# One transformer step with RWKV, linear attention and attention: the first RWKV batch is merged like the others, modulated rows are scaled at the residual, and turned modulation rows wait for the next ones

## The chip, the cores and the metric

The kernel runs on 1 core of one Trainium2 chip. The metric is device time in microseconds, from one launch, of that core. Three runs of the kernel before gave 2029.8, 2041.27 and 2041.91 us; their median is 2041.27 us.

## The reference

Two layers (`DEPTH = 2`) of a hybrid backbone run over 384 tokens: 128 context tokens and 256 latent tokens, each a row of 1024 channels. Cut to what matters:

```python
mod = silu(cond) @ w_ada + b_ada            # shift, scale and gate of both sub-layers
h = rms_norm(x, g_mix) * (1 + sc1) + sh1
p = h @ w_in
o_a = attention(...)                        # 8 heads, QK-norm, rotary
o_b = gated linear attention, forward + backward
o_c = RWKV-7 scan, forward + backward, group norm, gate
merged = sum of sigmoid(gate_i) * (o_i @ w_po_i)
x = x + gt1 * (merged @ w_out)
h2 = rms_norm(x, g_ffn) * (1 + sc2) + sh2
x = x + gt2 * ((silu(gu[:F]) * gu[F:]) @ w_ffn_out)
```

The outputs are the new rows of x and the context's keys, values and final states. All is float32; the six large projections are computed as three products of rounded halves (high x high, low x high, high x low).

## The kernel before

Channels lie on the 128 partitions and the 384 tokens along the free axis, so x and h are 8 tiles of 128x384. The program is written out by hand for each engine (`@block.tensor`, `@block.vector` and so on), and every hand-over is a semaphore; nothing is scheduled by a tool. A layer has five phases with a barrier behind each: (0) input projection, (1) attention, (2) gated linear attention, (3) RWKV, (4) output projection and feed-forward.

**Weights.** SyncE streams them in a fixed order into a ring of three slots of 1 MB. A slot is loaded again when its last user is done (`last_use`). The large projections split each arrived chunk into a high and a low half (ACT copies at L1361, DVE subtracts at L1816).

**Side work.** The matmuls of the branch gates (`gate`, L624, 8 matmuls of 128x384 in 4 steps), of the branch projections (`po`, L630, 4 matmuls in 2 steps) and of the modulation (`ada`, L621, one step each) have no place of their own: a generator `side_steps` hands them out in the order of `side_plan`, and the PE program calls `fill(n)` for n steps wherever it would wait. In RWKV the counts stand in the tuple `FILLS`, taken in turn by `fill(next(steps))`. The 48 steps of phase 3 are po 0 to 3 with gates between, four ada, po 4 to 7 with gates between, four ada. Two PSUM banks (6 and 7) serve all of it alternately, so a step that begins a new item waits until the item two before it is emptied. The side results are taken out by ACT (ada to `modrow`, L1340; gates, L1353) and by DVE (po, L1808 and L1810; modulation, L1801), each in `side_work`, which runs at fixed points of their programs, ahead of the next ordinary bank they take over.

An ada step gives 256 modulation values as a row; `turn_mod` (L603) turns them to columns by two small matmuls. `modrow` has two halves, so ACT takes row j only when row j-2 has been turned. The row is turned when more than two are held behind an ada item, and at once behind an item of another kind:

```python
while len(rows) > (2 if kind == "ada" else 0):
    turn_mod(*rows.pop(0))
```

**RWKV (phase 3).** The 8 heads go in 4 batches of 2 heads, n = 0 to 3, and each batch has both directions d = 0, 1 over 6 chunks of 64 tokens. For each of the 8 groups g = 2n + d DVE and ACT form decay terms (`logs` L2101 to L2105, `keys` L2113 to L2116, `terms` L2125 to L2137). Then follow for each batch: `grams` (PE L883, DVE L2146 to L2153), `begin` (DVE transpose L2159), a substitution on POOL (`substitution`, L1279 to L1286), `inverses` (DVE L2164, L2169, L2173), `merges` (PE L990 and L999 with DVE and ACT taking out each of the steps MM, QQ, SS, EE, FF), `factor` (PE L932, L943; DVE L2239; ACT L1604), `values` (PE L524, L958), `turned` (L969) and `read` (L990), `transitions` (PE L990 and L999), three `scan_step`s (PE L1034, DVE L2208) with fills between them, and `outputs` (PE L1047, L1053). For n = 1 and 2 factor, values, turned and read stand inside `merges`, where for n = 0 and 3 there are fills. For n = 0 they stand ahead of the loop, and for n = 3 at the end of batch 2.

**Norm.** The squares of x go to `squared` (for the first norm of a layer that is h itself; ACT, L1383), are summed over channels by ones-matmuls (L549), and ACT makes rstd in `gate[:, 0]` by Ln and Exp (L1391, L1393). DVE then makes h = x * scale * rstd for each of the 8 tiles in two pieces, 128 context and 256 latent columns, since the two have different scales (L1844); ACT writes the high half with the shift added (L1372) and DVE the low half (L1824). `residual` (L1855, L1856) adds gt * projection to x, one tile at a time, in the output projection and the second feed-forward projection.

## Time and profile before

| | us |
|---|---|
| runs, median of 3 | 2041.27 |
| the profiled execution | 2040.51 |
| its span, first to last instruction | 2038.7 |
| PE busy (90%) | 1826.6 |
| DVE busy (50%) | 1025.7 |
| ACT busy (36%) | 736.7 |
| POOL busy (7%) | 149.4 |

The phases are found in the trace by their lines. Layer 0: start to 48, input projection to 208, attention to 298, linear attention to 403, RWKV to 648, output and feed-forward to 1047 us. Layer 1: 1206, 1298, 1402, 1645 and the end. In the rows a line number is one of the kernel, "out<-in" are tiles, x is a count, and the bracket is the idle time of the engine just ahead with what ended it. PE rows may cover many matmuls; one float32 matmul is recorded as two instructions, so one step of a gate is x4. A busy time is no rate: at half the granted clock the same matmuls fill twice the time.

### The profile page before, as it was taken

Reading aid. Unit: us, or ns where it says so; the run is one execution under the profiler, and the core shown is the slowest. Engines: PE = TensorE matmul, PEld = TensorE weight load, DVE = VectorE, ACT = ScalarE, POOL = GpSimd, SP = SyncE. Lnnn points to the kernel's source line nnn. Section 1 sums busy time; section 2 is a strip of 40 time slices with the busy share of each in tenths; the row PEclk is TensorE's granted clock in tenths of the full one; section 3 lists DMA queues with packets and bytes.
Section 4 is the critical chain, followed back from the end, with each engine's and each line's share of the span. In section 5 each row is a group of like instructions: output and inputs, shape, how many; then the busy total and the mean of one; then the engine's idle time right before and its main releaser. Section 6 shows DMA issues by size and latency. Waiting matters only on the chain.

```text
span 2038.7 us, 38816 instructions
## 1 busy us (share of the span) xinstructions
PE 1826.6 (90%) x16819; PEld 1544.8 (76%) x16819; DVE 1025.7 (50%) x1827; ACT 736.7 (36%) x1297; POOL 149.4 (7%) x325
## 2 busy tenths in 40 slices
PE   5899898878796999999989989888687989999998
PEld 2899455546564989999989975555466669899998
DVE  1426438888544453333342444597775345533332
ACT  2334434333233343333243443523332333433321
POOL 2000000034110000000000000000522000000000
PEclk8899999989798999999999999999888989999999
DMA  7443231201304444663443433311012234344342
GB/s 259 166 127 114 89 110 47 81 9 44 105 3 145 145 135 131 185 166 106 128 134 106 126 96 100 111 51 47 2 61 89 84 117 127 94 126 130 112 116 85
DMA packets 267937, 214.48 MB, mean 105 GB/s; under 512 B 7226, under 2 KB 259545, under 8 KB 267513
## 3 DMA queue, kind: packets, MB, share of 16 engines
q1 hardware_dynamic: 264816, 204.41, 33.1%
q0 software_dynamic: 2736, 7.54, 1.2%
q8 instruction: 134, 2.20, 0.5%
q14 instruction: 35, 0.28, 0.0%
q10 hardware_dynamic: 216, 0.06, 0.0%
HBM read 209.10 MB, written 2.88 MB: 104 GB/s over the span
## 4 chain that ended last, share of the span: by engine, by line
PE 72%; DVE 17%; ACT 5%; issue 4%; DMA 1%; SPq 0%; ACTq 0%; POOL 0%; DVEq 0%; POOLq 0%
PE bank L565 12%; PE bank L570 12%; PE bank L566 12%; PE bank L624 8%; PE bank L1188 3%; PE bank L1186 3%; PE bank L1187 3%; PE bank L990 3%; DVE gate L2076 3%; PE bank L621 2%; PE bank L630 2%; PE bank L524 1%; PE bank L999 1%; PE bank L932 1%; PE bank L603 1%
## 5 line engine op out<-in xcount | busy, mean ns | idle before, releaser
L566 PE MATMUL bank<-scr_rounded 128*128 128x384 f32 x1344 | 453.6, 337 | 0.0
L566 PEld LDWEIGHTS bank<-scr_rounded 128*128 128x128 f32 x1344 | 254.9, 190 | 1.3
L565 PE MATMUL bank<-scr_rounded,gate_rounded 128*128 128x384 f32 (+1 forms) x672 | 229.0, 341 | 12.7 <-ACT scr_rounded L1372 9.5
L565 PE MATMUL bank<-scr_rounded 128*128 128x384 f32 (+1 forms) x672 | 227.0, 338 | 9.2 <-ACT scr_rounded L1372 8.7
L624 PE MATMUL bank<-h,ring 128*128 128x384 f32 x576 | 218.8, 522 | 10.9 <-DVEq L351 9.6
L570 PE MATMUL bank<-scr_rounded,gate_rounded 128*128 128x384 f32 (+1 forms) x672 | 223.2, 338 | 0.0
L570 PE MATMUL bank<-scr_rounded 128*128 128x384 f32 (+1 forms) x672 | 221.8, 336 | 0.0
L1816 DVE TENSOR_TENSOR scr_rounded<-ring,gate_rounded 128x2048 fp32r<-128x2048 f32 (+3 forms) x65 | 135.4, 2083 | 159.1 <-ACT gate_rounded L1361 158.4
L1816 DVE TENSOR_TENSOR scr_rounded<-ring,scr_rounded 128x2048 fp32r<-128x2048 f32 (+1 forms) x65 | 135.4, 2083 | 144.3 <-ACT scr_rounded L1361 143.7
L624 PEld LDWEIGHTS bank<-h,ring 128*128 128x128 f32 x576 | 108.7, 200 | 92.1 <-issue 38.0
L1361 ACT ACTIVATE gate_rounded<-ring 128x2048 fp32r<-128x2048 f32 (+3 forms) x65 | 113.6, 1747 | 153.2 <-PE bank L570 67.9
L1361 ACT ACTIVATE scr_rounded<-ring 128x2048 fp32r<-128x2048 f32 (+1 forms) x65 | 113.5, 1746 | 146.9 <-PE bank L570 84.5
L565 PEld LDWEIGHTS bank<-scr_rounded,gate_rounded 128*128 128x128 f32 (+1 forms) x672 | 127.9, 190 | 15.5 <-issue 11.0
L565 PEld LDWEIGHTS bank<-scr_rounded 128*128 128x128 f32 (+1 forms) x672 | 126.9, 189 | 10.9 <-issue 9.3
L570 PEld LDWEIGHTS bank<-scr_rounded,gate_rounded 128*128 128x128 f32 (+1 forms) x672 | 127.3, 190 | 0.5
L570 PEld LDWEIGHTS bank<-scr_rounded 128*128 128x128 f32 (+1 forms) x672 | 126.3, 189 | 0.6
L2380 DVE TENSOR_TENSOR arena<-bank,arena 128x384 f32<-128x384 f32 x44 | 24.5, 558 | 170.5 <-PE bank L570 166.5
L630 PE MATMUL bank<-arena,ring 128*128 128x384 f32 x256 | 97.4, 518 | 6.3 <-DVEq L351 4.1
L621 PE MATMUL bank<-ring,scond 128*2 128x256 f32 x768 | 57.7, 423 | 24.3 <-ACT modrow L1340 13.5
L630 PEld LDWEIGHTS bank<-arena,ring 128*128 128x128 f32 x256 | 47.4, 197 | 37.1 <-issue 12.3
L830 PEld LDWEIGHTS bank<-scr 64*128 64x128 f32 x672 | 42.1, 188 | 36.2 <-DVE scr L2058 21.6
L830 PE MATMUL bank<-scr 64*128 64x128 f32 x672 | 50.6, 287 | 18.5 <-DVE scr L2058 11.0
(386 smaller groups left out, 3180.0 us busy)
## 6 DMA issues: line engine op xcount, KB each, us to landing
ring<-in_w_in_dram SPq DMA_DIRECT2D x56, 1024.0 KB, 5.3
ring<-in_w_ada_dram SPq DMA_DIRECT2D x48, 1024.0 KB, 5.2
ring<-in_w_ffn_in_dram SPq DMA_DIRECT2D x88, 512.0 KB, 5.3
ring<-in_w_ffn_out_dram SPq DMA_DIRECT2D x32, 704.0 KB, 4.6
ring<-in_w_out_dram SPq DMA_DIRECT2D x8, 1024.0 KB, 5.0
ring<-in_w_po_a_dram SPq DMA_DIRECT2D x4, 1024.0 KB, 6.0
ring<-in_w_po_b_dram SPq DMA_DIRECT2D x4, 1024.0 KB, 6.2
ring<-in_w_po_c_dram SPq DMA_DIRECT2D x4, 1024.0 KB, 9.8
```

What stands on the lines that cost most here:

```text
L565: pe.matmul(o, w_hi[:, k, :], right[0][k], start=k == 0, stop=False)
L566: pe.matmul(o, w_lo[:, k, :], right[0][k], start=False, stop=False)
L570: ins = pe.matmul(o, w_hi[:, k, :], right[1][k], start=False, stop=k == nk - 1)
L621: ins = pe.matmul(b[strip:strip + 2, 0:256], scond[:, :, k], w[:, k, :], start=k < 4, stop=k >= 4)
L624: ins = pe.matmul(b[:, 0:T], w[:, k, 128 * (j % 2):128 * (j % 2) + 128], h[:, k, :], start=k == 0, stop=k == KD - 1)
L630: ins = pe.matmul(b[:, 0:T], w[:, k, 128 * (j % 4):128 * (j % 4) + 128], src[:, k, :], start=k == 0, stop=k == 3)
L830: ins = pe.matmul(b[:, CH * cc:CH * cc + CH], zc, zc, start=True, stop=True)
L990: ins = pe.matmul(pair[d][hr[cols(d, h)], 64 * c:64 * c + 64], left(d, h, r, c), right(d, h, r, c), start=True, stop=True)
L1186: pe.matmul(b[:, 0:T], w_hi[:, k, :], ff_hi[n], start=n == 0, stop=False)
L1187: pe.matmul(b[:, 0:T], w_hi[:, k, :], ff_lo[n], start=False, stop=False)
L1361: A(shaped(whi[m % 2], name, j), weights(l, name, j), ACT.Copy).then_inc(*tells("w_hi"))
L1816: tt(shaped(wlo[m % 2], name, j), weights(l, name, j), value(shaped(whi[m % 2], name, j)), sub).then_inc(*tells("w_lo"))
```

## The change

It has four parts.

1. **First batch.** factor, values, turned and read of n = 0 go into `merges`, as for n = 1 and 2 (`n in (1, 2)` becomes `n < 3`). On DVE `inverses(0)` moves from behind factor(0), grams(1) and logs(4) to right behind terms(3); `begin(n + 1)` leaves `inverses` and is written behind `grams(1)` and at the end of the batches. FILLS loses five entries and gains in others.
2. **Turned rows.** A row is turned only when more than two are held, whatever the kind of the item.
3. **Scaled rows.** `norm` is split: `scales` makes the scale of the channels, `scaled_rows` writes h = x * scale right behind each residual (and ahead of the first norm), and `norm` multiplies by rstd alone, one 128x384 operation per tile.
4. **Squares.** The first norm's squares go to the place of the high half of h in `scr`, since h now holds the scaled rows.

```diff
-        squared = [h, arena[:, 23:31, :]]
+        squared = [scr[:, 0:KD * T].rearrange("p (a b) -> p a b", a=KD), arena[:, 23:31, :]]
...
-        FILLS = (4, 4, 0, 2, 1, 1, 1, 0, 1, 1, 1, 2, 1, 1, 1, 1, 2, 2, 2, 1, 1, 2, 2, 2, 1, 1, 1, 2, 1, 1, 1, 2, 1, 1)
+        FILLS = (4, 4, 0, 2, 2, 2, 2, 1, 1, 1, 1, 2, 2, 2, 1, 1, 2, 2, 2, 1, 1, 1, 2, 1, 1, 1, 2, 1, 1)
...
-                    while len(rows) > (2 if kind == "ada" else 0):
+                    while len(rows) > 2:
                         turn_mod(*rows.pop(0))
...
-                    if n in (1, 2):
+                    if n < 3:
                         factor(n, 0)
...
-                factor(0, 0)
-                factor(0, 1)
-                values(0)
-                fill(next(steps))
                 grams(1)
                 loras(4)
-                fill(next(steps))
-                turned(0)
-                read(0)
                 fill(next(steps))
...
-            def norm(l, which):
+            def scales(l, which):
...
+            def scaled_rows(which, k):
+
+                sc = (sc1, sc2)[which]
+                dve.wait_ge(*last())
+                for cols, n in ((slice(0, CH), 0), (slice(CH, T), 1)):
+                    ts(h[:, k, cols], x[:, k, cols], sc[:, k, n:n + 1], None, mult).then_inc(*step())
+
+            def norm(l, which):
+
+                dve.wait_ge(*last())
                 dve.wait_ge(S["rstd"], told("rstd", l, which + 1))
-                dve.wait_ge(*last())
                 for k in range(KD):
-                    for cols, n in ((slice(0, CH), 0), (slice(CH, T), 1)):
-                        ins = stt(out=h[:, k, cols], in0=x[:, k, cols], scalar=sc[:, k, n:n + 1], in1=gate[:, 0, cols], op0=mult, op1=mult)
-                        ins.then_inc(*(tells("normed") if n else step()))
+                    tt(h[:, k, :], h[:, k, :], gate[:, 0, :], mult).then_inc(*tells("normed"))
...
                     side_work("in", l, 0)
+                    scales(l, 0)
+                    for k in range(KD):
+                        scaled_rows(0, k)
                     split(first_split)
...
-                factor(0, 0)
-                factor(0, 1)
+                inverses(0)
                 grams(1)
+                begin(1)
                 logs(4)
-                inverses(0)
...
+                scales(l, 1)
                 for k in range(KD):
                     residual(l, k, ("out", l, k), 16)
+                    scaled_rows(1, k)
...
                     residual(l, k, ("ffo", l, k), 40)
+                    if l + 1 < layers:
+                        scaled_rows(0, k)
```

On ACT the same calls of factor, values, turned and read for n = 0 move from ahead of the loop (around `decays(4)`) into `merges(0)`.

On DVE, in RWKV of layer 0, right behind the last operation of terms(3) (L2137), stands before (L2239 and L2243 are factor(0), L2146 to L2153 grams(1), L2101 to L2105 logs(4), L2164 to L2173 inverses(0), L2159 begin(1)):

```order
L2239 TENSOR_TENSOR gate<-bank,cst 128x384 x8
L2243 TENSOR_SCALAR scr<-scr,small 128x64 x2
L2146 TENSOR_TENSOR cst<-bank,cst 128x384 x2
L2151 SCALAR_TENSOR_TENSOR lora<-cst 128x384
L2153 SCALAR_TENSOR_TENSOR cst<-lora,cst 128x12x16
L2101 SCALAR_TENSOR_TENSOR scr<-cst,arena 128x384
L2103 TENSOR_TENSOR scr<-scr 128x384
L2105 TENSOR_TENSOR scr<-scr,arena 128x384
L2164 STREAM_TRANSPOSE scr<-cst 128x16x32
L2169 TENSOR_TENSOR scr<-scr,cst 128x384 x2
L2173 STREAM_TRANSPOSE scr<-cst 128x16x32
L2159 STREAM_TRANSPOSE cst<-cst 128x512
```

and now (L2137 is the end of terms(3)):

```order
L2137 TENSOR_TENSOR scr<-arena,scr 128x6x64
L2164 STREAM_TRANSPOSE scr<-cst 128x16x32
L2169 TENSOR_TENSOR scr<-scr,cst 128x384 x2
L2173 STREAM_TRANSPOSE scr<-cst 128x16x32
L2146 TENSOR_TENSOR cst<-bank,cst 128x384 x2
L2151 SCALAR_TENSOR_TENSOR lora<-cst 128x384
L2153 SCALAR_TENSOR_TENSOR cst<-lora,cst 128x12x16
L2159 STREAM_TRANSPOSE cst<-cst 128x512
L2101 SCALAR_TENSOR_TENSOR scr<-cst,arena 128x384
L2103 TENSOR_TENSOR scr<-scr 128x384
L2105 TENSOR_TENSOR scr<-scr,arena 128x384
```

The eight products and two scalings of factor(0) have gone into the merge, inverses(0) comes first, and begin(1) stands ahead of logs(4).

On PE at the same place (L624 and L630 are side steps, L883 grams(1), L862 loras(4), L969 turned(0), the first L990 of each piece read(0) before; the next ones MM and QQ of batch 0, L999 SS) stands before:

```order
L624 MATMUL bank<-h,ring 128x384 x2
L883 MATMUL bank<-scr 64x64 x24
L862 MATMUL bank<-arena,lora 128x384 x2
L630 MATMUL bank<-arena,ring 128x384 x2
L969 MATMUL bank<-cst,scr 64x64 x24
L990 MATMUL bank<-arena,gate 64x64 x24
L990 MATMUL bank<-arena,scr 64x64 x24
L990 MATMUL bank<-scr,arena 64x64 x24
L630 MATMUL bank<-arena,ring 128x384 x2
L999 MATMUL bank<-scr,cst 64x64 x24
L624 MATMUL bank<-h,ring 128x384 x2
```

and now (L932 and L943 are factor(0)):

```order
L624 MATMUL bank<-h,ring 128x384 x4
L883 MATMUL bank<-scr 64x64 x24
L862 MATMUL bank<-arena,lora 128x384 x2
L630 MATMUL bank<-arena,ring 128x384 x4
L990 MATMUL bank<-arena,scr 64x64 x24
L990 MATMUL bank<-scr,arena 64x64 x24
L932 MATMUL bank<-scr 64x128 x24
L943 MATMUL bank<-cst,scr 64x64 x24
L999 MATMUL bank<-scr,cst 64x64 x24
L932 MATMUL bank<-scr 64x128 x24
L943 MATMUL bank<-cst,scr 64x64 x24
```

MM and QQ follow grams(1), loras(4) and two side steps; factor(0) has the place of the fills between QQ, SS and EE.

On PE at the end of batch 1 (L1034 scan steps, L621 ada, L603 turned rows, L1047 and L1053 outputs(1), L883 grams(3), L630 po) stands before:

```order
L621 MATMUL bank<-ring,scond 2x256 x16
L1034 MATMUL bank<-scr 64x64 x4
L621 MATMUL bank<-ring,scond 2x256 x8
L603 MATMUL bank<-cst,modrow 128x2 x2
L621 MATMUL bank<-ring,scond 2x256 x8
L603 MATMUL bank<-cst,modrow 128x2 x2
L1047 MATMUL bank<-gate,arena 64x64 x24
L1053 MATMUL bank<-scr 64x64 x20
L630 MATMUL bank<-arena,ring 128x384 x2
L883 MATMUL bank<-scr 64x64 x24
L630 MATMUL bank<-arena,ring 128x384 x2
L603 MATMUL bank<-cst,modrow 128x2 x4
```

and now (its first L624 is the fill behind the second scan step):

```order
L1034 MATMUL bank<-scr 64x64 x4
L624 MATMUL bank<-h,ring 128x384 x4
L1034 MATMUL bank<-scr 64x64 x4
L621 MATMUL bank<-ring,scond 2x256 x16
L1047 MATMUL bank<-gate,arena 64x64 x24
L1053 MATMUL bank<-scr 64x64 x20
L621 MATMUL bank<-ring,scond 2x256 x8
L603 MATMUL bank<-cst,modrow 128x2 x2
L883 MATMUL bank<-scr 64x64 x24
L621 MATMUL bank<-ring,scond 2x256 x8
L603 MATMUL bank<-cst,modrow 128x2 x2
```

All side items come two steps later than before, two ada follow one another with no turned row between them, and the four turned-row matmuls behind the last po step are gone.

## Rows read from the trace of the kernel before

**Rows 1.** Stages of layer 0: stretch, us, busy of PE, PEld, DVE, ACT, POOL, clock, DMA, GB/s.

```profile
403.00:648.00 245.00, 198.65 (x4163) 143.82 (x4164) 152.25 (x314) 79.36 (x192) 59.55 (x134) 0.90 0.21 67
648.00:1047.00 399.00, 388.18 (x2263) 371.17 (x2263) 166.90 (x206) 139.77 (x162) 1.45 (x2) 0.98 0.49 140
```

**Rows 2.** Waits of PE, RWKV stage of layer 0 (us in total, times, longest).

```profile
PE bank L990 <- issue: 8.7, 8, 3.1
PE bank L932 <- DVE gate L2239: 8.0, 1, 8.0
PE bank L603 <- DVE gtmp L1808: 5.2, 1, 5.2
```

**Rows 3.** Timeline, DVE, batch 0 (start us, us, engine line op [idle before]).

```profile
443.60 0.64 DVE L2137 TENSOR_TENSOR scr<-arena,scr 128x384 f32<-128x384 f32 x1
...
453.15 1.02 DVE L2146 TENSOR_TENSOR cst<-bank,cst 128x384 f32<-128x384 f32 x2 [3.48 <-PE bank L883]
...
454.87 0.56 DVE L2153 SCALAR_TENSOR_TENSOR cst<-lora,cst 128x192 f32<-128x192 f32 x1
...
458.73 1.06 DVE L2164 STREAM_TRANSPOSE scr<-cst 128x512 f32<-128x512 f32 x1
459.83 1.03 DVE L2169 TENSOR_TENSOR scr<-scr,cst 128x384 f32<-128x384 f32 x2
```

**Rows 4.** Timeline, POOL, the end of the first substitution.

```profile
444.77 0.24 POOL L1286 TENSOR_TENSOR cst<-cst,lora 128x28 f32<-128x28 f32 x1
```

**Rows 5.** Timeline, PE, grams(1) and batches 0 and 1 of layer 0.

```profile
452.16 0.93 PE L883 MATMUL bank<-scr 64*64 64x64 f32 x48
...
460.91 0.93 PE L990 MATMUL bank<-arena,scr 64*64 64x64 f32 x48 [2.61 <-DVE scr L2169]
...
477.43 2.85 PE L624 MATMUL bank<-h,ring 128*128 128x384 f32 x8
480.21 0.68 PE L1034 MATMUL bank<-scr 64*64 64x64 f32 x16
...
496.52 1.20 PE L990 MATMUL bank<-cst,scr 64*64 64x64 f32 x48 [1.95 <-DVE scr L2169]
...
524.30 0.68 PE L1034 MATMUL bank<-scr 64*64 64x64 f32 x16
```

**Rows 6.** Timeline, PE, from the scan of batch 1 to batch 2.

```profile
526.77 1.91 PE L621 MATMUL bank<-ring,scond 128*2 128x256 f32 x32
...
537.61 2.83 PE L1047 MATMUL bank<-gate,arena 128*64 128x64 f32 x48
...
552.50 1.56 PE L990 MATMUL bank<-arena,scr 64*64 64x64 f32 x48
```

**Rows 7.** Timeline, DVE, the same stretch.

```profile
534.08 0.55 DVE L2137 TENSOR_TENSOR scr<-arena,scr 128x384 f32<-128x384 f32 x1
```

**Rows 8.** Timeline, PE, the last batch (3) of layer 0.

```profile
614.90 0.93 PE L990 MATMUL bank<-cst,scr 64*64 64x64 f32 x48
...
623.30 1.89 PE L621 MATMUL bank<-ring,scond 128*2 128x256 f32 x16 [1.91 <-DMA ring<-in_w_ada_dram]
...
637.80 1.05 PE L621 MATMUL bank<-ring,scond 128*2 128x256 f32 x16
...
641.63 0.68 PE L1034 MATMUL bank<-scr 64*64 64x64 f32 x16
...
645.06 1.62 PE L1047 MATMUL bank<-gate,arena 128*64 128x64 f32 x48 [0.66 <-DVE scr L2208]
```

**Rows 9.** Timeline, the first norm of the program, DVE and PE.

```profile
54.73 1.41 DVE L1844 SCALAR_TENSOR_TENSOR h<-x,sc,gate 128x128 f32<-128x128 f32 x4
...
56.46 0.66 PE L565 MATMUL bank<-scr_rounded 128*128 128x384 f32 x1 [4.45 <-ACT scr_rounded L1372]
```

**Rows 10.** Groups of one form, DVE, scalar times one tile (busy us, mean ns).

```profile
L1977 DVE TENSOR_SCALAR scr<-scr,small 128x128 f32<-128x128 f32 x16 | 4.6, 287 | 0.6
```

**Rows 11.** Timeline, ACT, one pair of attention blocks.

```profile
271.04 0.49 ACT L1353 ACTIVATE mg<-bank 128x384 f32<-128x384 f32 x1 [0.62 <-PE bank L624]
```

27 lines of the change are left out of this document (13 added, 14 removed).

## The prediction

> **What bounds the kernel now.** I read the times by stage first. PE is at work in nine tenths of the span, but the RWKV stages fall out: 245 us in layer 0 with PE busy 198.65 and a mean granted clock of 0.90, against 388.18 of 399 us and 0.98 in the stage behind it [rows 1]. Layer 1 has 243 us for the same work. So some 46 us a layer are idle there, and part of the busy time ran at 1.2 instead of 2.4 GHz. A change of PE's order can win there and hardly elsewhere. The waits of PE name the idle time: 8.0 us once on DVE's factor products, 5.2 us once because a turned row wanted a side bank that DVE had not emptied, and 8.7 us "issue", which no order mends [rows 2]. The timelines then show three weak places, and every number below is of layer 0. The two layers run the same program there, so I double it.
>
> **First batch.** DVE ends terms(3) at 444.2 [rows 3] and POOL the first substitution at 445.0 [rows 4]. Before, inverses(0) stands behind factor(0), grams(1) and logs(4): its transpose starts at 458.73 and its two products end at 460.9 [rows 3], where MM of batch 0 starts [rows 5]. Some 13.7 us of that are only order. Now DVE waits 0.8 us for POOL, needs 2.1 us as in rows 3, and MM is released at 447.2. But PE is not there: at 444.2 it begins grams(1), 0.93 us [rows 5], then loras(4), as wide as one side step, and two side steps, 2.85 us [rows 5], with loras(4) taken as 1.45. That is 449.5 at full clock. PE has waited 10 us by then, so I add 1.5 us for a slow start (the L1047 group took 2.83 us at 537.61 after such waits [rows 6], and 1.62 us at 645.06 [rows 8]). MM starts at 451.0. DVE is not late for QQ: grams(1) ends 2.3 us after it begins [rows 3], begin(1) and logs(4) cost some 3 us more, so DVE is there at about 454, 1 us behind PE.
>
> From MM to the first scan step, batch 0 took 480.21 - 460.91 = 19.3 us without factor and batch 1 took 524.30 - 496.52 = 27.8 us with it [rows 5]. Batch 0 will look like batch 1, less the slow clock that PE had there (its MM group took 1.20 us, that of batch 0 0.93 [rows 5]): I take 26.2 us. The first scan step comes at 477.2 instead of 480.21: **3 us a layer won**, with bounds of 1 (27.8 us, MM at 451.5) and 6 (24 us, MM at 450). The 9.9 us gained at MM are nearly all given back inside the merge.
>
> **End of batch 1.** From the scan's side steps at 526.77 to MM of batch 2 at 552.50 pass 25.7 us [rows 6], though DVE ends terms of the last group at 534.6 [rows 7]. Four ada, each held by the next turned row, fill it up to 537.61 [rows 6], and the 5.2 us wait follows [rows 2]. Now: two gate steps 2.85, a scan step 0.3, an ada 1.0 (the pair takes 1.91 [rows 6]) and a second one that waits until ACT has taken out the gate, which stands behind ACT's exponentials: I put its end at 532.5. Outputs 2.9 (a 1.62 group and one about as long less a fifth [rows 8]), 535.4. An ada and its turned row 1.5, grams(3) 0.93, 537.8. DVE then needs 2.3 for grams(3) with 0.2 for a modulation row, and 2.1 for inverses(2) [rows 3]: MM at 542.4. **9.9 us won a layer**; DVE bounds it from above (534.6 + 0.9 + 2.3 + 2.1 = 539.9, 12.6 us). From below I take 4, if the third ada waits 6 us for its weights: its slot comes free only with the last gate step, at 529.5, and in the last batch an ada in the same place did wait for DMA [rows 8].
>
> **Last batch.** From MM at 614.90 to outputs at 645.06 pass 30.2 us [rows 8], with the DMA wait at 623.30 in the middle of the merge, which stops DVE as well. Two steps later, the last po ends at the third fill of the merge, and the ada that needs its slot runs behind the transitions, some 9 us on; that wait goes. The merge then is batch 0's of before, 19.3 us with gate steps where now two ada with two turned rows stand (637.80 to 641.63, 3.8 us, for 2.85 [rows 8, 5]): 20.3 us. The last two ada fall between the scan steps, which before took 3.4 us [rows 8]; with them some 6.4 us, as the last one's slot comes free only with the first ada. 26.7 us: **3.5 us won a layer**, bounds 0 (the 3.1 us "issue" stall of this stage [rows 2] stays and the last ada waits longer) and 7.
>
> **Attention.** The turned row now comes right behind its ada, and the next gate takes the ada's own bank. ACT empties it only behind the exponentials of the pair: it took out a gate at 271.04 for scores of 267.3 [rows 11], 3.7 us, while scores, ada and turned row cost PE 2.4 us. Two such places a layer cost 1.3 us each; I **add 2 us a layer** (0 to 3). In linear attention there is one step at a time and room between; I count nothing, and up to 1 us a layer if ACT is late there.
>
> **First norm.** Its 16 multiplications stand between the last modulation row and the split, and nothing covers them: PE waited 4.45 us for ACT's first high tile [rows 9], and all of that lengthens. One of 128 columns takes 287 ns [rows 10]; one of 256 lies between that and the 480 ns or so of the product of two tiles (four products of 128 and 256 columns take 1.41 us [rows 9], 0.33 us each start to start). With the wait ahead of each pair I take 0.57 us a pair, 4.6 us; bounds 3.5 and 5.5. The Trainium skill (VectorE: DVE Perf Modes, The DRAIN you can't avoid) says that each operation flushes the pipeline anyway and a semaphore between two costs nothing more. By that the wait is free and the sum 0.8 us lower. The trace does not bear it out for operations without a wait: 0.33 us from start to start of products that last up to 0.48 us overlap.
>
> **Later norms and residuals.** One operation of 384 columns stands where two were ahead of the first high tile. Half of the 1.41 us group [rows 9] is 0.7 us, one product of 384 columns takes 0.51 us (two in 1.02 [rows 3]): 0.2 us for each of three norms, **0.6 us won**. The tiles behind it don't count, since PE needs longer than DVE for each. The 24 pairs of multiplications behind residuals cost DVE 0.57 us each beside the large projections, a stage in which DVE is idle for 232 of 399 us [rows 1]: nothing, and at most 0.6 us for each last one (1.8 us in all) if the sum of squares didn't cover it. The squares' new place costs nothing.
>
> **Sum.** Own time of the profiled execution 2040.51 us, 0.8 us below the median of the runs. Won 2 x (3 + 9.9 + 3.5) + 0.6 = 33.4; added 4.6 + 2 x 2 = 8.6. 2040.5 - 24.8 = **2015.7 us**.
>
> **Rivals.**
> (A) DVE is the bound of the batches, and what PE wins at the end of batch 1 is lost again. For it: DVE is busy 152 of 245 us there [rows 1], more than elsewhere. Against: at the end of batch 1 DVE had done its terms 18 us ahead of MM [rows 7, 6]. Then only 4 instead of 9.9 and 1 instead of 3: 2015.7 + 2 x 7.9 = 2031.5 us.
> (B) Nothing comes of it, since side steps only move (their sum is the same) and the slow clock moves with them: gains of 1, 4 and 0 a layer give 2040.5 - 10 - 0.6 + 8.6 = 2038.5 us.
> (C) Slower: an ada now takes a side bank right behind another item, so PE waits for ACT or for weights at many of the 32 ada of phases 1 to 3, not at two a layer. At 1.3 us each, the attention's price, they cost 41.6 us in place of the 4: 2015.7 + 37.6 = 2053 us. It decides from 0.9 us for each (24.8 + 4 = 28.8 over 32). For it: the bank rule; against: most ada stand at fills with one step, where ACT is idle.
> (D) The merge with factor in batch 0 pays no give-back: all 9.9 us stay. 2015.7 - 13.8 = 2002 us. Against: batch 1's row.
>
> **How the numbers follow.** A measurement of this kernel tells a difference of about 1%. Forecast with its own band (2006 to 2021): 0.55; A 0.24; B 0.08; C 0.05; D 0.08. Faster by over 1% means below 2020.9: nearly all of the forecast and D, 0.63. Same: A, B, a part of C and of the forecast's upper edge, 0.34. Slower than 2061.7 needs C at 1.6 us each: 0.03. The range reaches down to 1998 (D, and all upper bounds of the last two places) and up to 2033 (A).
>
> **What would show it.** Right: MM of batch 0 some 10 us earlier against terms(3), but the first scan step only 1 to 6; no wait of L603 on L1808's successor; MM of batch 2 at about 13 us less distance; the wait for `in_w_ada` gone from batch 3; an RWKV stage of 226 to 232 us; the first L565 matmul at 61. Wrong: an RWKV stage above 240, new waits of L603, L621 or L624 on ACT of over 5 us in attention, or DVE without idle time ahead of inverses(2).

## The result, and the profile after

The changed kernel takes **2030.24 us** (median of 20 runs, 2019.45 to 2033.11) against 2041.97 us of the kernel before in the same comparison (20 runs). The ratio is 0.9941, with the interval 0.9931 to 0.9952: a gain of 0.6% (11.7 us), where 1.2% was forecast (24.8 us less than the profiled execution before, 2015.7 us). The profiled execution took 2032.43 us, its span is 2030.6 us, 8.1 below the span of before.

The time was won in the RWKV stage, as forecast, but only half as much of it. Here are the stretches of layer 0 (columns: stretch, us, busy time of PE, PEld, DVE, ACT, POOL, granted clock, DMA share, GB/s). They are not cut as [rows 1], which ends the stage at 648 us, just behind the outputs of batch 3. Here it ends at the first gate step of the next stage, 651.91 us; in the kernel before that step comes at 658.32. So the first row is the kernel before, cut in the new way (254.3 us, not 245), and the other two are the kernel after:

```profile
404.10:658.40 254.30, 202.20 (x4201) 146.10 (x4201) 155.58 (x319) 85.22 (x201) 60.42 (x135) 0.90 0.20 64
408.50:652.00 243.50, 197.65 (x4203) 143.03 (x4202) 154.59 (x318) 85.36 (x201) 59.72 (x135) 0.91 0.20 64
652.00:1051.00 399.00, 388.90 (x2241) 371.24 (x2242) 174.70 (x233) 141.53 (x165) 3.74 (x7) 0.98 0.51 145
```

On the cut of [rows 1] the stage of layer 0 fell from 245 to some 236 us, between the two signs that the forecast had set (226 to 232 for right, above 240 for wrong).

To compare term by term I cut the stage at events that both kernels have: the stage's first output step on PE, the first scan step of batches 0 and 1, MM of batch 2, the outputs of batch 2, the first gate step of the next stage. In the table are us from event to event, layer 0 / layer 1.

| stretch | before | after | forecast a layer | measured a layer |
|---|---|---|---|---|
| start to scan of batch 0 | 75.5 / 76.7 | 74.2 / 74.3 | -3 | -1.8 |
| to scan of batch 1 | 44.1 / 44.8 | 43.9 / 45.7 | 0 | +0.4 |
| to MM of batch 2 | 28.2 / 27.1 | 18.7 / 20.9 | -9.9 | -7.8 |
| to outputs of batch 2 | 32.8 / 32.0 | 33.5 / 32.1 | 0 | +0.4 |
| to the next stage's gate | 73.0 / 69.7 | 72.4 / 71.4 | -3.5 | +0.5 |
| the stage | 253.6 / 250.2 | 242.8 / 244.4 | -16.4 | -8.3 |

Over both layers the stage is 16.6 us shorter where 32.8 were forecast. The rest of the span got 8.5 us longer, where 8.0 were forecast (first norm 4.6, attention 4, later norms -0.6).

The events themselves in PE's timeline of the kernel after, layer 0, first to last (start us, us, engine line op):

```profile
409.16 2.26 PE L630 MATMUL bank<-arena,ring 128*128 128x384 f32 x3 [0.37 <-DVEq L351]
...
483.35 0.68 PE L1034 MATMUL bank<-scr 64*64 64x64 f32 x16
...
527.29 0.68 PE L1034 MATMUL bank<-scr 64*64 64x64 f32 x16
...
546.02 1.56 PE L990 MATMUL bank<-arena,scr 64*64 64x64 f32 x48 [1.92 <-DVE scr L2169]
...
579.50 1.62 PE L1047 MATMUL bank<-gate,arena 128*64 128x64 f32 x48
...
651.91 2.90 PE L624 MATMUL bank<-h,ring 128*128 128x384 f32 x4 [4.16 <-DVEq L351]
```

PE's waits in that stage, the answer to [rows 2] (us in total, times, longest). The 8.0 us wait on the factor products is gone and so is the 5.2 us wait of L603; a wait of 13.3 us on the terms stands where the first was. The line to look at is the second: "issue" is time in which PE waited for nothing that the profile shows. In L990 it went from 8.7 us [rows 2] to 10.4. Over all lines of the stage it went from 11.6 to 12.8 us in layer 0, and from 5.9 to 14.8 us in layer 1.

```profile
PE bank L883 <- DVE scr L2137: 14.5, 2, 13.3
PE bank L990 <- issue: 10.4, 8, 3.7
```

The first norm, answering to [rows 9], DVE and then PE (the first two rows are DVE's):

```profile
51.63 4.64 DVE L1835 TENSOR_SCALAR h<-x,sc 128x128 f32<-128x128 f32 x16
56.18 2.28 DVE L1804 TENSOR_TENSOR scr_rounded<-ring,scr_rounded 128x2048 fp32r<-128x2048 f32 x1
...
60.04 0.66 PE L565 MATMUL bank<-scr_rounded 128*128 128x384 f32 x1 [8.92 <-ACT scr_rounded L1365]
```

The 16 multiplications take 4.64 us (4.6 forecast), PE's wait is 8.92 instead of 4.45 us, and its first matmul comes at 60.04 instead of 56.46 us.

### The profile page after: what moved, and what is told of

Read it like the earlier page. It is cut to its first block, busy times and chain, and to the rows that moved or that the text cites. A ratio compares the mean times of both kernels' runs of the same rounds, so it can differ in the third digit from the quotient of the medians.

```text
span 2030.6 us, 38851 instructions
## 1 busy us (share of the span) xinstructions
PE 1819.7 (90%) x16819; PEld 1537.5 (76%) x16819; DVE 1036.8 (51%) x1859; ACT 736.9 (36%) x1297; POOL 148.0 (7%) x325
## 4 chain that ended last, share of the span: by engine, by line
PE 73%; DVE 16%; ACT 5%; issue 4%; POOL 1%; DMA 1%; SPq 0%; ACTq 0%; DVEq 0%; POOLq 0%
PE bank L565 12%; PE bank L570 12%; PE bank L566 12%; PE bank L624 7%; PE bank L1181 3%; PE bank L1180 3%; PE bank L1179 3%; PE bank L990 3%; DVE gate L2076 3%; PE bank L630 2%; PE bank L621 2%; PE bank L524 1%; PE bank L999 1%; PE bank L603 1%; PE bank L932 1%
## 5 line engine op out<-in xcount | busy, mean ns | idle before, releaser
L565 PE MATMUL bank<-scr_rounded,gate_rounded 128*128 128x384 f32 (+1 forms) x672 | 228.9, 341 | 11.8 <-ACT scr_rounded L1365 9.3
L565 PE MATMUL bank<-scr_rounded 128*128 128x384 f32 (+1 forms) x672 | 227.0, 338 | 13.6 <-ACT scr_rounded L1365 13.0
L624 PE MATMUL bank<-h,ring 128*128 128x384 f32 x576 | 213.3, 515 | 11.7 <-DVEq L351 8.3
L624 PEld LDWEIGHTS bank<-h,ring 128*128 128x128 f32 x576 | 108.7, 198 | 91.0 <-issue 33.3
L1354 ACT ACTIVATE gate_rounded<-ring 128x2048 fp32r<-128x2048 f32 (+3 forms) x65 | 113.6, 1747 | 153.1 <-PE bank L570 67.9
L565 PEld LDWEIGHTS bank<-scr_rounded,gate_rounded 128*128 128x128 f32 (+1 forms) x672 | 127.7, 190 | 14.6 <-issue 10.8
L565 PEld LDWEIGHTS bank<-scr_rounded 128*128 128x128 f32 (+1 forms) x672 | 127.0, 189 | 15.2 <-issue 13.7
L2381 DVE TENSOR_TENSOR arena<-bank,arena 128x384 f32<-128x384 f32 x44 | 24.5, 558 | 173.3 <-PE bank L570 166.7
L630 PE MATMUL bank<-arena,ring 128*128 128x384 f32 x256 | 102.3, 539 | 0.7 <-DVEq L351 0.7
L630 PEld LDWEIGHTS bank<-arena,ring 128*128 128x128 f32 x256 | 49.0, 204 | 35.1 <-issue 12.1
L830 PEld LDWEIGHTS bank<-scr 64*128 64x128 f32 x672 | 42.0, 187 | 42.3 <-DVE scr L2058 28.5
L621 PE MATMUL bank<-ring,scond 128*2 128x256 f32 x768 | 54.6, 407 | 15.9 <-ACT modrow L1333 8.0
```

The lines of the kernel that those rows point to most:

```text
L565: pe.matmul(o, w_hi[:, k, :], right[0][k], start=k == 0, stop=False)
L621: ins = pe.matmul(b[strip:strip + 2, 0:256], scond[:, :, k], w[:, k, :], start=k < 4, stop=k >= 4)
L624: ins = pe.matmul(b[:, 0:T], w[:, k, 128 * (j % 2):128 * (j % 2) + 128], h[:, k, :], start=k == 0, stop=k == KD - 1)
L630: ins = pe.matmul(b[:, 0:T], w[:, k, 128 * (j % 4):128 * (j % 4) + 128], src[:, k, :], start=k == 0, stop=k == 3)
L830: ins = pe.matmul(b[:, CH * cc:CH * cc + CH], zc, zc, start=True, stop=True)
L1354: A(shaped(whi[m % 2], name, j), weights(l, name, j), ACT.Copy).then_inc(*tells("w_hi"))
```

## What "issue" is: the first reading of the two traces

The last batch was to gain 3.5 us a layer and gained nothing, though its wait for `in_w_ada` [rows 8] is gone. PE's timeline of batch 3 after:

```profile
620.04 1.63 PE L990 MATMUL bank<-scr 64*64 64x64 f32 x96 [1.47 <-DVE scr L2227]
622.00 0.93 PE L990 MATMUL bank<-gate,scr 64*64 64x64 f32 x48 [0.32 <-ACT scr L1619]
622.72 0.74 PE L990 MATMUL bank<-arena,scr 64*64 64x64 f32 x34
627.16 0.70 PE L990 MATMUL bank<-arena,scr 64*64 64x64 f32 x14 [3.69 <-issue]
627.79 2.83 PE L999 MATMUL bank<-arena 128*64 128x64 f32 x48
630.54 1.89 PE L621 MATMUL bank<-ring,scond 128*2 128x256 f32 x16
```

PE stops for 3.69 us in the middle of a group (34 matmuls, then the other 14 of the same 48), with nothing to wait for, and then runs at half the clock: L999 takes 2.83 us for what takes 1.6. The DMA view of three stretches around it, with its queues (packets, MB, share of 16 engines), shows what happens. First 504.9 to 528 us, the merge of batch 1; then 618.5 to 624.6; then 624.6 to 626:

```profile
q8 instruction: 6, 0.10, 1.7%
q1 hardware_dynamic: 60, 0.05, 0.7%
...
q1 hardware_dynamic: 1899, 1.93, 98.1%
...
q1 hardware_dynamic: 171, 0.16, 37.0%
q8 instruction: 1, 0.02, 5.2%
```

Queue q8 brings PE its instructions. I read this from the counts, 134 packets of 16 KB in the whole trace for the 33,638 records of PE and PEld, 251 for each, and from the times below. I call such a packet a block. In the merge of batch 1 one block comes each 3.4 to 4.3 us (they start at 504.97, 509.00, 513.30, 517.13, 520.99 and 524.37 us), and the small "issue" stalls of 0.7 to 1.6 us in the merges end 2.2 to 2.7 us behind the start of such a block (the group after the one of 517.13 goes on at 519.67). In the last batch a block starts at 617.02 and the next only at 624.69, and in between two modulation weight loads of 1 MB each fill all 16 engines (98.1%). SP issued them at 617.75 and 618.16 us. PE stands from 623.5 to 627.16, again 2.5 us behind the start of the late block.

The 3.1 us stall of [rows 2] was already of this kind. In the kernel before, layer 0, a block starts at 624.37 and the next at 631.63, with 2.4 MB of loads between them, and PE goes on 2.4 us later:

```profile
634.01 0.38 PE L990 MATMUL bank<-gate,scr 64*64 64x64 f32 x4 [3.08 <-issue]
```

In layer 1 of that kernel the batch had no such stall (0.3 us of issue in all) but a longer wait for `in_w_ada`, 3.12 us. After the change the wait is gone in both layers and a stall of 3.69 or 3.51 us stands in both.

The Trainium skill (Advanced Engine Details and Errata, ISA Cache) says that instructions are held in lines of 16 KB, 256 instructions; the packets agree with that. How many such lines there are no row here shows. The Trainium skill (DMA: Bandwidth & Descriptors, Queues, rings and completion order) says that a DMA engine takes turns between its queues packet by packet. By that a block would wait only briefly behind the loads. The trace doesn't bear a brief wait out: 7.7 us between two blocks instead of some 4. Where in between the block waited, in its queue or ahead of it, no row shows.

So there were two theories. **Theory 1**, the forecast's: PE's order and DVE decide, the issue time is a constant. **Theory 2**: the dense merges (some 780 small matmuls with their weight loads, six blocks) are bound by the supply of instructions, and a weight load that falls between two blocks delays the later one, and PE with it.

## Experiments

All ratios are to the kernel before, run on the same chip. Runs of one kernel differ: six of the kernel `hold` lay between 2019.9 and 2035.0 us, with mean granted clocks of 0.962 and 0.955. Medians of 4 to 10 runs are therefore good to some 3 us, and the stage lengths of the profiled execution say more on a single term. But that execution can lie at either end of its kernel's runs, so I lean on a stretch only where several kernels with the same edit agree on it.

**The first norm alone put back.**

```diff
-                    tt(h[:, k, :], h[:, k, :], gate[:, 0, :], mult).then_inc(*tells("normed"))
+                    if l == 0 and which == 0:
+                        for cols, n in ((slice(0, CH), 0), (slice(CH, T), 1)):
+                            ins = stt(out=h[:, k, cols], in0=x[:, k, cols], scalar=sc1[:, k, n:n + 1], in1=gate[:, 0, cols], op0=mult, op1=mult)
...
-                    for k in range(KD):
-                        scaled_rows(0, k)
                     split(first_split)
```

> The changed kernel with one part undone: in the first norm of the program the product x * scale * 1/rms is made in one operation again, the other three norms stay as changed. Theory 1 (the prediction's, the 16 multiplications stand uncovered ahead of the first split): the split starts some 4.1 us earlier (52.1 instead of 56.3 us) and all that stands behind it follows, 2030.2 - 4.1 = 2026.1 us. Rival (a later wait of the start, for the projections' weights or for ACT, swallows it): 2029 to 2030.5 us, with a longer wait of L565 in the first projection.

Measured: 2028.11 us, ratio 0.9939 (0.9921 to 0.9957), the profiled execution 4.9 us below that of the changed kernel, of which 1.6 stand at the first L565 (58.49 against 60.04 us, as this execution reached its wait 2.9 us later). PE's wait is back to its old size:

```profile
58.49 0.66 PE L565 MATMUL bank<-scr_rounded 128*128 128x384 f32 x1 [4.50 <-ACT scr_rounded L1365]
```

The median moved by 2 us only, within its uncertainty. In the trace the term is 4.4 us (wait 4.50 against 8.92), close to the 4.6 forecast, and the time does not contradict it.

**The first batch and the table of side steps put back.** The diff is the RWKV part of the change, reversed; the rule of the turned rows and the norms stay changed.

> The changed kernel with the first RWKV batch and the table of side steps as before; the new turn rule and the scaled rows stay. Theory 1 (the prediction's terms): the first batch loses its 3 us and the last batch its 3.5 us a layer, 2030.2 + 13 = 2043 us. Theory 2 (the batches are bound by the supply of PE's instructions, blocks of 256 that come 3.4 to 4 us apart): what the merged first batch won was about 1 us a layer and the last batch nothing, so 2030 to 2033 us, and the stalls marked issue on L990 and L999 in batch 0 fall from some 4.4 us to under 1.5 us a layer.

Measured: 2039.8 us, ratio 0.9988 (0.9971 to 1.0006). Without this part nothing is won. That is near theory 1's number (2043) and far from theory 2's, but both had left out the end of batch 1, where most of it is: MM of batch 2 comes 25.2 and 25.0 us behind the scan's first step, not 18.7 and 20.9. The first batch gives back 2.2 us a layer, the last 1.5, not 3.5, so that theory 1 is near by luck. The stalls of batch 0 did fall, to 0.6 and 1.3 us, as theory 2 had it. The stage is 250.4 and 250.7 us long.

**The old rule for the turned rows.**

```diff
-                    while len(rows) > 2:
+                    while len(rows) > (2 if kind == "ada" else 0):
```

> The changed kernel with the old rule for the modulation rows (a row is turned before the next gate or output step is taken out of the list). Theory 1 (the prediction's): the end of batch 1 loses its 9.9 us a layer, attention gets back 1.3 us a layer: 2030.2 + 19.8 - 2.6 = 2047 us, with the 5.2 us wait of L603 back. Rival (the end of batch 1 is won by the shifted side steps, not by the rule): 2027 to 2031 us.

Measured: 2029.77 us, ratio 0.9942 (0.9922 to 0.9962), no different from the changed kernel. The rival holds. From the first scan step of batch 1 to MM of batch 2 it takes 18.7 and 18.4 us, and PE's timeline there has the same order as that of the changed kernel; two adas stand ahead of the outputs, two behind, and no turned row is held up:

```profile
535.97 1.05 PE L621 MATMUL bank<-ring,scond 128*2 128x256 f32 x16
537.60 1.05 PE L621 MATMUL bank<-ring,scond 128*2 128x256 f32 x16 [0.58 <-ACT gtmp L1346]
538.57 1.62 PE L1047 MATMUL bank<-gate,arena 128*64 128x64 f32 x48
...
545.57 1.05 PE L621 MATMUL bank<-ring,scond 128*2 128x256 f32 x16 [1.41 <-DMA ring<-in_w_ada_dram]
548.99 1.56 PE L990 MATMUL bank<-arena,scr 64*64 64x64 f32 x48 [1.84 <-DVE scr L2169]
```

With batch0_old this makes a table of four for that stretch (mean of the layers): neither part 27.7 us, the rule alone 25.1, the order alone 19.2 (order_only, below), both 19.8. So the order and the shifted side steps win all of it, and the rule, which alone won 2.6 us, adds nothing to them. That it is the shift and not batch 0's order shows in fill_early below: with two steps shifted back this stretch takes 23.9 us, 4 more. Attention, from its first gate step to linear attention, takes 91.5 us a layer with the old rule (mean of four kernels) and 92.8 with the new (fourteen): the rule costs 1.3 us a layer. PE's waits in attention of layer 0 show it, in the kernel before and then in the changed one; the gate now waits until ACT has emptied the ada's bank:

```profile
PE bank L624 <- ACT mg L1353: 0.7, 2, 0.3
```

```profile
PE bank L624 <- ACT modrow L1333: 1.7, 2, 1.1
```

**The weight loads of the last adas made small.**

```diff
+                elif name == "ada" and 20 <= j < 24:
+                    sp.dma_start(dst[:, 0:1, :], source(l, name, j)[:, 0:1, :]).then_inc(w_arrived[n % NSLOT], 16)
```

> The changed kernel with seven eighths of the last four modulation weight loads of each layer left out (128 KB instead of 1 MB each; the matrices multiply what lay in the buffer). Nothing else moves. In the last batch PE stands still for 3.7 us (layer 0) and 3.5 us (layer 1) in L990, with no engine waited for, and two of these loads (2 MB) run over all DMA engines just then, between two blocks of PE's instruction queue that come 7.7 us apart instead of 3.4 to 4. Theory 2 (the loads hold up PE's instructions): that stall falls to under 1.2 us in both layers and the groups behind it run at the full clock, 2.5 to 4.5 us a layer, 2021 to 2025 us. Rival (the stall belongs to the place in the program, or to DVE): the stall stays over 3 us and the time at 2029 to 2031 us.

This kernel leaves seven eighths of these weights out and so computes something else, in the changed kernel's order of work. The changed kernel has no wait for weights in that batch, so that the traffic is what differs.

Measured (4 runs): 2019.67 us, ratio 0.9893 (0.9859 to 0.9926), 10.6 us less than the changed kernel. The block behind 619.34 now comes after 5.2 us, and the stall is:

```profile
626.95 0.46 PE L990 MATMUL bank<-arena,scr 64*64 64x64 f32 x14 [0.68 <-issue]
627.33 1.62 PE L999 MATMUL bank<-arena 128*64 128x64 f32 x48
```

0.68 us for 3.69 (0.95 for 3.51 in layer 1), and L999 at the full clock. From MM to the first scan step of batch 3 it takes 20.5 and 20.7 us instead of 26.05 and 24.5, and from the outputs of batch 2 to the next stage it takes 66.8 and 67.0 us instead of 72.4 and 71.4. Theory 2 holds for the last batch: 5 us a layer are the collision's, the stall and the slow clock behind it together.

**Side steps into the merge of batch 1.** In `merges` a fill stands behind the second factor group, the values and the read; in batch 1 they do one step each and the three fills behind it one instead of two.

> The changed kernel with three side steps moved in batch 1 alone: one each behind the second factor group, the values and the read of its merge, taken from the fills behind its transitions and its first two scan steps (2, 2, 2 become 1, 1, 1). The stretch from MM of batch 1 to its first scan step gets two side steps more on balance, 2.9 us of matmuls, and the stretch from there to the outputs two fewer. Theory 2 (the merge is bound by the supply of instructions, a side step brings few of them, 8 for 1.45 us): the first stretch stays within 1 us of its 27.7 and 29.4 us, the second falls from 8.2 to some 5.5 us, the stalls marked issue in batch 1 fall from 2.1 and 2.4 us below 1, and the time is 2024 to 2027 us. Rival (PE's own work or DVE bounds the merge): the first stretch grows by 2.9 us and the time stays at 2029 to 2031 us.

Measured: 2030.7 us, ratio 0.9949 (0.9928 to 0.9971). From MM to the first scan step it takes 27.9 and 28.5 us with two more side steps in it, against 27.7 and 29.4: they cost nothing there, and the rival's 2.9 us are not to be seen. The room came from the issue time (1.2 and 0.4 us instead of 2.1 and 2.4), as theory 2 has it, and for the rest from elsewhere: a granted clock of 0.94 instead of 0.88 in layer 0, 1.2 us less of waiting for ACT in layer 1. From there to the outputs 6.2 and 6.9 us instead of 8.2. But the 1 to 2 us that were won came back in front of MM of batch 2, where grams(3) stalls for instructions (1.95 us in layer 0, 1.87 in layer 1; 0 and 2.3 in the changed kernel). The local effect was as forecast, the total (2024 to 2027) was not.

**Side steps spread over all merges.**

> The changed kernel with its side steps in other places: two steps that stood between loras(4) and MM of batch 0 go ahead of grams(1), where PE waits 13 us for DVE's last terms; one step each goes into the merges of batches 0 and 1 at three places and into that of batch 2 at one; scan steps get one step each instead of two. Theory 2 (supply): MM of batch 0 comes 4 us or more earlier against the stage's start, the merges grow by under 1.5 us each, an RWKV stage of 233 to 238 us instead of 243.6, 2010 to 2019 us in all. Theory 1 (side steps only move, as rival B had it, and only the two ahead of grams(1) are covered): 2024 us. What could spoil it: weight loads that fall into another dense stretch (stalls of over 2 us on issue).

Measured: 2037.52 us, ratio 0.9983 (0.9969 to 0.9997), slower than the changed kernel, and the expectation (2010 to 2019) missed by some 20 us. The adas came to stand inside the merge of batch 1, which took 36.5 us from MM to scan (34.9 in layer 1). PE's waits from 495 to 540 us:

```profile
PE bank L989 <- issue: 2.5, 2, 1.9
PE bank L942 <- DVE scr L2216: 2.1, 1, 2.1
PE bank L621 <- ACT modrow L1332: 2.0, 1, 2.0
```

An ada brings a wait for ACT's row, and its 1 MB load fell between the blocks (6.3 us from block to block there). Room in the merge of batch 1 was free for gate and output steps (fill_one), not for adas. The same with the first norm put back:

> The side steps as in fill_merge and the program's first norm made in one operation as before the change. The two edits stand in different stages: the time of fill_merge less 4.1 us for the norm, 2006 to 2015 us.

Measured: 2033.61 us, ratio 0.9965 (0.995 to 0.9979), 3.9 us less than fill_merge, the norm's term once more; the number expected missed with that of fill_merge.

**Two steps more in the 13 us wait.** In the table the fifth entry becomes 4 instead of 2, the last two 0 instead of 1.

> The changed kernel with two side steps more ahead of grams(1), in PE's 13 us wait for DVE's last terms, and none between the last batch's scan steps. Both theories: the two steps are covered there (2.9 us a layer) and PE is back at the full clock sooner for the two steps ahead of MM of batch 0 (they took 4.2 instead of 2.9 us), and all later steps come two places earlier, so that the last batch's weight loads fall elsewhere. 2.9 us a layer alone: 2024.4 us; with the clock 2022 us. Theory 2 adds that the stalls of over 3 us in the last batch move or go: as low as 2016 us; theory 1 has no such term.

Measured: 2034.16 us, ratio 0.9967 (0.995 to 0.9984), 10 us above what both theories had expected. The scan of batch 0 comes 1.5 us a layer sooner, but all later steps shift by two, all four adas stand between the scan and the outputs of batch 1 again, where the third waits 2.4 us for ACT's row (11.8 us from scan to outputs of batch 1 instead of 8.2), and the stall of the last batch stays (3.63 and 2.75 us).

**The two loads held back.**

```diff
+                if (name, j) == ("ada", 21):
+                    sp.wait_ge(psum_ready, filled("VZ", l, 3, 1))
```

> The changed kernel, all of its work kept, with one wait more on SP: in each layer the two modulation weight loads that collided with PE's instruction blocks in the last batch (ada 21 and 22, issued 0.4 us apart at 617.75 and 618.16) are held until PE has issued the VZ group of batch 3. Theory 2 (the loads hold up the instructions): the stall of L990 behind FF falls from 3.7 and 3.5 us to some 1 us and the groups behind it are at the full clock, as when the loads were left out: batch 3 reaches its first scan step 3.5 to 5 us sooner a layer, 2030.2 - 7 to 10 = 2020 to 2023 us. What could take it back: the second ada of the pair waits for its weights, up to 2 us a layer (2025 us). Rival: the stall is not of the loads' making and stays, and the late weights cost 2 us a layer, 2034 us.

Measured: 2025.0 us (6 runs), ratio 0.9929 (0.9903 to 0.9955), what the expectation had given with late weights; its trace is of the slowest of the six (2035.03 us). The stall is 0.95 and 0.77 us, and the first scan step of batch 3 comes 5.4 and 4.0 us sooner behind the outputs of batch 2. But up to the next stage all of that is lost again (72.5 and 72.1 us in all). The expectation had named a wait for weights. PE's timeline of this execution shows none:

```profile
635.52 0.68 PE L1034 MATMUL bank<-scr 64*64 64x64 f32 x16
...
641.02 1.89 PE L621 MATMUL bank<-ring,scond 128*2 128x256 f32 x16
642.84 1.02 PE L603 MATMUL bank<-cst,modrow 128*128 128x2 f32 x4
643.79 2.83 PE L1047 MATMUL bank<-gate,arena 128*64 128x64 f32 x48
646.55 2.40 PE L1053 MATMUL bank<-scr 64*64 64x64 f32 x40
```

The next block had to wait instead (8.1 us from block to block, 2.2 MB of loads between), PE stalled 1.1 us inside the scan step, and everything behind it ran at half the clock: L1047 2.83 us, where it is 1.62 in the changed kernel. With the first norm put back, and then with the old rule for the rows too:

> The changed kernel with the held loads and the first norm of the program in one operation. The two stand in different stages: the time of hold less 3 to 4.1 us, 2016 to 2020 us.

> As hold_norm, with the old turn rule too. The turn rule was worth nothing in turn_old (2029.8 against 2030.2 us); attention gets back 1.3 us a layer by the forecast's term, the last batch's rows then stand in one place again: within 3 us of hold_norm, rather below it, 2014 to 2020 us. If the rule matters once the collision is gone, it is over 4 us slower.

Measured: 2023.77 us, ratio 0.9905 (0.988 to 0.993), and 2022.25 us, 0.9913 (0.9884 to 0.9942). The rule makes no difference that can be measured here either. Both lie 2 to 4 us above what was expected (up to 2020 us). Their traces show the same loss behind the scan: from its first step to the outputs 7.6 to 10.8 us instead of the changed kernel's 5.0 (5.7 and 6.0 in turn_old), with a mean clock from that step to the next stage of 0.68 to 0.78 in the three kernels instead of 0.94 and 0.97. But in layer 0 of these two a wait for weights does stand there (0.34 and 1.03 us in hold_norm, 0.33 and 0.99 in hold_norm_turn):

```profile
635.67 1.89 PE L621 MATMUL bank<-ring,scond 128*2 128x256 f32 x16 [1.03 <-DMA ring<-in_w_ada_dram]
```

So what the hold gave back was in part the moved collision and in part late weights; the slow clock stands behind either.

**The order of the batches alone.** The kernel before with the RWKV part of the change (the first batch and the table of side steps) and nothing else.

> The kernel before with the order of the first RWKV batch and the table of side steps alone taken from the change; the turn rule and the four norms stay as before. turn_old gave 2029.8 us with this order and all norms changed. Theory: the change's whole gain is this part, and the first norm's 4.1 us are given away on top, the later norms win 0.6: 2029.8 - 4.1 + 0.6 = 2026.3 us. Rival (the norms' multiplications behind the residuals shift the phases and cost or win more elsewhere): outside 2023 to 2030 us.

Measured: 2027.17 us, ratio 0.9937 (0.9916 to 0.9958). This part makes the whole gain (2026.3 us was expected); the rule and the norms together add nothing that can be measured.

**Two loads in the other order.** With the loads' order the ring's three buffers are dealt out differently: ada 21 gets the buffer of gate 7, which is free earlier, and only ada 22 is left to wait for that of po 3.

```diff
+        for l in range(layers):
+            m, n = order.index((l, "po", 3)), order.index((l, "gate", 7))
+            order[m], order[n] = order[n], order[m]
```

> The changed kernel with two neighbouring weight loads of SP's list in each layer in the other order (po 3 and gate 7). The ring's buffers are given out in that order, so that the load of ada 21 now waits for gate 7's buffer, free some 25 us ahead of batch 3, and only ada 22 waits for po 3's and falls into the merge: 1 MB there instead of 2. Theory 2: the stall behind FF falls from 3.7 and 3.5 us to between 1 and 2.5 us, and nothing behind it waits for weights: 2 to 4 us a layer, 2022 to 2027 us. Rival (any load there costs the full stall, since the block waits for a place and not for the bytes): stall over 3 us, 2030 us.

Measured: 2023.72 us, ratio 0.9909 (0.9881 to 0.9938). ada 21 is issued at 611.95 us, ahead of MM (10 us earlier, not 25), ada 22 at 621.67. The stall (four lines more ahead make L990 to L994 and L999 to L1003):

```profile
628.47 0.45 PE L994 MATMUL bank<-arena,scr 64*64 64x64 f32 x14 [1.09 <-issue]
628.86 1.33 PE L1003 MATMUL bank<-arena 128*64 128x64 f32 x38
```

The stall is 1.09 and 1.23 us, MM to scan takes 20.9 and 21.0 us, and from the outputs of batch 2 to the next stage it is 67.4 and 67.9 us: 4.3 us a layer, nearly all that leaving the loads out had won. All work is kept. The trace is of the fastest of the five runs, but the two kernels below with the same swap agree (67.5 and 67.7, 68.9 and 67.4).

> As swap, with the one load left in the merge (ada 22) held until PE has issued the VZ group of batch 3, and the first norm in one operation. No load is left ahead of VZ, and the held one is needed 10 us later: the stall falls below 1.2 us as in hold, and the 3 us a layer that hold gave back between the last scan steps don't come: 2030.2 - 8 to 9.4 - 3 to 4.1 = 2017 to 2019 us, against 2023.8 us of hold_norm. If it is no better than hold_norm, what hold gave back was not the late weights of ada 21.

Measured: 2019.01 us, ratio **0.9899** (0.9878 to 0.9919), the fastest kernel that does all the work: 22 us under the kernel before, and its interval lies wholly below that of the changed kernel (0.9931 to 0.9952). It has the swap, the hold and the old first norm. Its last stretch is 67.5 and 67.7 us, so that the hold adds nothing to the swap.

**The two side steps ahead of MM of batch 0.** They go into its merge, behind the second factor group and the values.

> The changed kernel with the two side steps that stand between loras(4) and MM of batch 0 (4.2 us at the slow clock) moved into the merge of batch 0, one behind the second factor group and one behind the values; all later steps stay in their places. MM can then start at about 452.6 instead of 456.7 us. Theory DVE-then-supply: DVE is busy with grams(1), begin(1) and logs(4) until 458.4 us whatever PE does, takes QQ at 459.5 us as now, and from there the supply of instructions sets the pace and swallows the two steps: the first scan step moves by no more than 1 us either way (74.2 us from the stage's start), the total stays at 2028 to 2031 us, and the stalls marked issue of batch 0 fall from 4.4 to some 2 us. Theory 1 (PE's late arrival cost the missing 2 us of the forecast's first term): the first scan step 2 to 4 us sooner, 2022 to 2026 us. Rival: the steps add to the merge, 1 to 2 us slower a layer, 2033 us.

Measured: 2035.42 us, ratio 0.9975 (0.9958 to 0.9993), slower than the changed kernel and nearest to the rival's number (2033). The profiled execution was the fastest of the ten (2026.79 us), so the trace does not show what made the others slow, and that stays open. What it shows of batch 0 is this. MM comes at 453.23 instead of 456.73 us, and PE then waits for DVE's QQ:

```profile
460.30 1.56 PE L942 MATMUL bank<-cst,scr 64*64 64x64 f32 x48 [2.86 <-DVE scr L2216]
```

In the changed kernel that wait is 1.03 us, and the rows of DVE there say why it could not be less: grams(1), begin(1) and logs(4) come first.

```profile
452.18 1.02 DVE L2146 TENSOR_TENSOR cst<-bank,cst 128x384 f32<-128x384 f32 x2
...
454.48 0.71 DVE L2159 STREAM_TRANSPOSE cst<-cst 128x512 f32<-128x512 f32 x1
455.12 1.70 DVE L2101 TENSOR_TENSOR_SCAN scr<-cst,arena 128x384 f32<-128x384 f32 x1
...
459.54 1.01 DVE L2217 TENSOR_TENSOR scr<-bank,cst 128x384 f32<-128x384 f32 x2
```

The first scan step is 75.3 and 74.3 us from the stage's start, against 74.2 and 74.3: two side steps more in the merge, issue time in it 1.7 instead of 4.4 us in layer 0, and the first scan step within 1.1 us of where it was, as the first theory of the expectation had it; its total (2028 to 2031) is missed. The same edit on top of swap_hold_norm:

> swap_hold_norm with the side steps of fill_zero. They stand in different batches: the time of swap_hold_norm plus the difference that fill_zero makes (0 by the first theory, -4 to -8 by theory 1).

Measured: 2024.11 us, ratio 0.9915 (0.9885 to 0.9945), 5.1 us above swap_hold_norm, as fill_zero is 5.2 above the changed kernel. The edit costs 5 us in both, which neither theory had. Here the traces do show a place: the RWKV stages are 3.7 and 3.6 us longer than in swap_hold_norm (241.9 and 242.7 against 238.2 and 239.1), 1.1 and 3.4 us of it ahead of the first scan step. In fill_zero's fast execution the stages are within 1.1 us of the changed kernel's, so that the cause stays open.

## Where the forecast was right and where it failed

**End of batch 1, -9.9 forecast, -7.8 measured.** Right in place and nearly in size: 9.5 in layer 0, 6.2 in layer 1, where grams(3) stalled 2.3 us on issue. (The forecast's own terms end at 542.4, which is 10.1 us and not 9.9.) Wrong in its cause in one point: the text had the turned rows' rule and the shifted steps together; the four kernels and fill_early show that the shift does it without the rule. With it two adas instead of four stand ahead of the outputs of batch 1, so that none waits for a row's turn (2.4 us where four stand, in batch0_old and fill_early).

**First norm, +4.6 forecast.** The multiplications cost 4.64 us and PE's wait grew by 4.5; the first matmul came 3.6 us later, since DVE's last modulation row was 0.9 us early in this execution. Right.

**Attention, +2 a layer.** 1.3 us by the kernels with either rule. Within its bounds of 0 to 3.

**First batch, -3 forecast, -1.8 measured.** "MM starts at 451.0" is 4 us later in this kernel, for terms(3) ends later by that; MM came at 456.73, 1.7 us behind that. The slow clock lasted through grams(1), loras(4) and both side steps: 8.5 us from the start of grams(1), where the forecast had 5.2 and 1.5 added once. I would have called this the missing part, and fill_zero says it is not: DVE is at QQ at 459.5 us, and at 459.1 there with MM 3.5 us earlier. "DVE is there at about 454, 1 us behind PE" is the same number (458 here) and should have been carried on as the bound. Behind it the merge took 26.6 us from MM to scan (26.2 forecast), 4.4 of it issue.

**Last batch, -3.5 forecast, +0.5 measured.** This is the failed step: 8 of the 16.7 us by which the profiled execution missed (4.2 are the end of batch 1, 2.4 the first batch). The forecast called the issue time something "which no order mends". It let the wait for `in_w_ada` go and put nothing in its place; what stood there was a stall of 3.69 and 3.51 us, where before it was 3.08 and 0.3. It saw the 3.1 us stall of this stage [rows 2] and used it only for the lower bound of this term, as if its size were given. It priced the merge at 20.3 us, batch 0's 19.3 and the adas. It was 26.05 from MM to the scan (609.23 to 635.28), and 24.5 in layer 1. The price itself was good: without the collision it is 20.5 and 20.7 us (ada_small) or 20.9 and 21.0 (swap). The loads that PE no longer waited for ran at another time, across PE's own instructions. The wait for `in_w_ada` (1.91 us [rows 8], 3.12 in layer 1) was exchanged for a longer stall with the slow clock behind it. ada_small and swap show that 4 to 5 us a layer were to be had there.

In the forecast's own stretch, from MM to the outputs of batch 3, it is 31.0 and 29.5 us, against 30.2 and 27.4 before and 26.7 forecast. So the miss is larger there than in the table, whose stretch goes on to the next stage and got 1.6 and 0.4 us shorter behind the outputs. And doubling layer 0 was a second slip: layer 1 stood at 27.4 us already, so that 26.7 would have won 0.7 us there and not 3.5.

With the collision gone (swap), the stage's last stretch is 3.8 us a layer shorter than before. That this is near the forecast's 3.5 is in part luck: it is 5.7 us in layer 0, from which the 3.5 were worked out, and 1.8 in layer 1.

**Rival A** named 2031.5 us, close to what came, by luck: its mechanism isn't what happened, since DVE kept only a small part, at the first batch. Rival C's 32 waits came to nothing: over the whole program L621 waits 8.0 us for ACT's rows, 13.5 before, and only L624's waits for ACT grew, from 1.3 to 3.3 us. Of the other 2 us of the miss, 1.6 are the two stretches of the table that were forecast at 0; they are not explained.

## What to carry to other kernels

Read "issue" gaps of PE against the instruction queue before you call them fixed. In a stretch of many small matmuls ask when the next block comes, and keep megabyte loads out of it; with a ring of few buffers, two neighbouring loads in the other order can be enough. And ask for each wait on a transfer that goes what else the transfer will run across when it is no longer waited for.

Side steps with few instructions and long matmuls can be free inside a stretch that is short of instructions: two were in the merge of batch 1. Moving them also moves every later step and load, so that one such step can't be priced alone.

## What I had not expected of the hardware

- In the merge of batch 1 PE got one block of some 250 instructions each 3.4 to 4.3 us; a group of 48 matmul records of 64 columns with its weight loads runs in 0.74 us, so that a block lasts it about 2 us at that pace (an estimate from these two). Whether the queue could bring blocks faster, no run shows.
- Two 1 MB loads, 98.1% of the 16 engines for 6 us, held a 16 KB block back by some 4 us; with one 1 MB load there (swap) the blocks are 6.0 us apart and the stall is 1.1 us.
- After a stall of 3.69 us the next 5 us ran at half the clock (granted clock 0.50 from 627.2 to 632.4 us, L999 2.83 us, L621 1.89), after one of 0.68 us they didn't (L999 1.62). In hold a stall of 1.13 us inside the scan had the slow clock behind it too (0.51 from 640 to 649 us), and in swap one of 1.09 us in the middle of the merge had not.
